# A decoder layer on eight cores: residual loaded into the accumulators, a seventh weight slab, split first loads, the last norm in halves

## The reference

```python
b_gate, c_gate, hc, q, k, v, g = split(x @ w_in)           # 512 columns each
y_conv = b_gate * causal_short_conv(c_gate * hc, conv_w)   # 3 taps
q, k = rotary(q), rotary(k) * 128 ** -0.5
o = chunkwise_retention(q, k, v)                           # 4 heads, chunks of 128
y_ret = silu(g) * head_group_norm(o)
x = layer_norm(ALPHA * x + concat([y_conv, y_ret]) @ w_out)
ff = square(relu(x @ w_ff1)) @ w_ff2                       # 1024 -> 4096 -> 1024
ple = sigmoid(x @ w_ple_gate) * (p @ w_ple_proj)
x = layer_norm(ALPHA * x + ff + ple)
```

## Time and profile before

| what | value |
|---|---|
| median of 6 runs | 891.23 us |
| profiled execution | 891.71 us |
| its span (first to last instruction, slowest core) | 890.1 us |
| spans of the eight cores | 880.8 to 890.1 us |
| mean granted TensorE clock of the cores | 0.972 to 0.980 |
| TensorE busy | 810.1 us (91%) |
| VectorE (DVE), ScalarE (ACT), GpSimd (POOL) busy | 443.9, 277.6, 147.4 us |
| moved by DMA | 128.41 MB, mean 144 GB/s |

### The profile page before, as it was taken

One profiled execution on the slowest core, in us unless ns is written; L12 is line 12 of the kernel. 1 busy time (PEld: TensorE's weight loads), 2 busy tenths in 40 slices (PEclk: granted clock), 3 DMA queues, 4 the chain that ended last, 5 costly groups with the idle time before them and its releaser, 6 DMA issues.

```text
span 890.1 us, 12563 instructions; the slowest of 8 cores (880.8 to 890.1 us)
## 1 busy us (share of the span) xinstructions
PE 810.1 (91%) x4088; PEld 375.8 (42%) x4088; DVE 443.9 (50%) x696; ACT 277.6 (31%) x500; POOL 147.4 (17%) x205
## 2 busy tenths in 40 slices
PE   1999999999878999659999999999999999999990
PEld 0444444444444444214444444444444444444440
DVE  4458544556754345124268454437653436844153
ACT  2222236545566333002234312214320322431010
POOL 2000145544454200001001000101100101100010
PEclk9999999999999999859999999999999999999995
DMA  8993599962367999968476877567787667784311
GB/s 134 218 173 53 104 165 108 123 108 59 48 103 135 147 195 183 178 126 144 139 176 182 220 181 180 125 167 171 201 197 189 134 151 140 215 208 108 88 48 47
DMA packets 21999, 128.41 MB, mean 144 GB/s; under 512 B 2800, under 2 KB 2928, under 8 KB 10224
## 3 DMA queue, kind: packets, MB, share of 16 engines
q0 software_dynamic: 11856, 83.37, 55.0%
q1 hardware_dynamic: 10080, 44.25, 14.8%
HBM read 194.19 MB, written 18.87 MB: 239 GB/s over the span
## 4 chain that ended last, share of the span: by engine, by line
PE 67%; DMA 11%; DVE 7%; issue 5%; ACT 4%; POOL 4%; DVEq 0%; ACTq 0%; POOLq 0%; SPq 0%
PE ps L194 65%; DMA xin_117<-x 5%; DMA ring_104<-w_gate 4%; DMA wc_59<-wc 2%; ACT sqj L223 2%; DVE lnst L673 2%; POOL st_51 L201 1%; DVE xacc_119 L201 1%; PE psT L198 1%; DVE xacc_118 L201 1%; ACT xacc_119 L223 1%; POOL lnst L201 1%; DVE ra_80 L201 1%; ACT xacc_118 L223 1%; DVE ob_93 L201 0%
## 5 line engine op out<-in xcount | busy, mean ns | idle before, releaser
L223 ACT ACTIVATE xacc_119<-xacc_119,lnst 128x1024 f32<-128x1024 f32 x16 | 19.8, 1240 | 133.9 <-DVE lnst L212 133.9
L194 PE MATMUL ps<-ring_106,hT 128*128 128x512 bf16 x160 | 42.7, 429 | 15.5 <-DVE xacc_119 L212 15.5
L201 POOL TENSOR_TENSOR lnst<-lnst,neghalf 128x1 f32<-128x1 f32 x32 | 17.9, 561 | 163.9 <-DVE lnst L205 163.8
L201 DVE TENSOR_TENSOR hT<-ps,tR_128 128x512 bf16<-128x512 f32 x43 | 29.6, 689 | 29.9 <-ACT tR_128 L223 29.8
L194 PE MATMUL ps<-ring_108,hT 128*128 128x512 bf16 x192 | 43.2, 379 | 0.7 <-DVE xacc_119 L212 0.7
L194 PE MATMUL ps<-ycat,ring_107 128*128 128x512 bf16 x192 | 43.6, 383 | 0.0
L194 PE MATMUL ps<-ring_109,hT 128*128 128x512 bf16 x192 | 43.2, 379 | 0.0
L194 PE MATMUL ps<-ycat,ring_106 128*128 128x512 bf16 x192 | 42.9, 379 | 0.3 <-DMA ring_106<-w_ff 0.3
L201 DVE TENSOR_TENSOR hT<-ps,tR_129 128x512 bf16<-128x512 f32 x42 | 28.9, 689 | 28.4 <-ACT tR_129 L223 28.3
L201 DVE TENSOR_TENSOR hT<-ps,tR_127 128x512 bf16<-128x512 f32 x43 | 29.6, 689 | 26.1 <-ACT tR_127 L223 24.5
L223 ACT ACTIVATE tR_127<-ps 128x512 f32<-128x512 f32 x43 | 25.7, 598 | 53.2 <-PE ps L194 49.0
(11 more groups left out here) (268 smaller groups left out, 1459.4 us busy)
## 6 DMA issues: line engine op xcount, KB each, us to landing
ring_106<-w_ff POOLq DMA_DIRECT2D x11, 1024.0 KB, 9.7
ring_108<-w_ff POOLq DMA_DIRECT2D x11, 1024.0 KB, 9.2
ring_104<-w_ff POOLq DMA_DIRECT2D x10, 1024.0 KB, 9.4
ring_109<-s_ff SPq DMA_DIRECT2D x9, 1024.0 KB, 5.3
s_ff<-w_ff POOLq DMA_DIRECT2D x8, 1024.0 KB, 29.8
ring_105<-s_ff SPq DMA_DIRECT2D x8, 1024.0 KB, 5.7
ring_107<-s_ff SPq DMA_DIRECT2D x7, 1024.0 KB, 5.2
ring_107<-w_ff POOLq DMA_DIRECT2D x4, 1024.0 KB, 20.9
```

The source lines that it names most:

```text
L194: self.P.op("pe", lambda e: e.matmul(out, lhsT=lhsT, rhs=rhs, start=start, stop=stop, skip_group_check=skip), reads, writes)
L201: self.P.op(eng, lambda e: e.tensor_tensor(out=out, in0=in0, in1=in1, op=op), reads, writes)
L223: self.P.op("act", lambda e: e.activation(out=out, in_=in_, func=func, **kw), reads, writes)
```

## The change

`xin` is used by tile 0 alone. For tiles 1 to 3, x is loaded by SP into `xacc` itself, one DMA per block of 128 rows, and `mix_part` works in place; tile 1's loads are issued before the channel stage, those of tile tt + 2 from `gen_out(tt, bi)` behind the output DMAs that free the rows. The ring gets a seventh buffer on the bytes of `xin`, and loads go up to 6 slabs ahead. Four casts are put ahead of the first three slab loads. The first two `xT` tiles and `wc` groups are loaded in quarters along the contraction (`wc` is laid out anew for that), and the first four conv steps take their matmuls in the order of the pieces, the third and fourth step in alternation. For the last tile the norm is made by four fused operations on half rows, with statistics of the first half made after its own sum and one output DMA per half, on SP and on ACT.

```diff
-    NR = 6
-    ring_off = [o_wc, o_wc + 8 * KB, o_wc + 16 * KB, o_xT + 16 * KB, o_xT + 24 * KB, o_sin]
+    NR = 7
+    ring_off = [o_wc, o_wc + 8 * KB, o_wc + 16 * KB, o_xT + 16 * KB, o_xT + 24 * KB, o_sin,
+                o_cb + 8 * KB]
...
-        cast(xT[0][:], xTd[0], ("xT", 0), ("xT", 0))
-        cast(wc[0][:], wcd[0], ("wc", 0), ("wc", 0))
...
+        for k in range(4):
+            load_part(0, 0, k)
+            load_part(1, 0, k)
+        for kind, i in ((1, 1), (0, 1), (1, 2), (1, 3), (0, 2), (0, 3)):
+            for k in range(len((xT_res, wc_res)[kind][i])):
+                load_part(kind, i, k)
...
-        slab_buf = [0, 1, 2, 3, 0, 1, 4, 5]
+        slab_buf = [0, 1, 2, 3, 0, 1, 6, 4, 5]
         while len(slab_buf) < len(slab_list):
-            slab_buf.append(slab_buf[-6])
+            slab_buf.append(slab_buf[-7])
...
+            order = [(gi, kc) for gi in (2, 1, 0) for kc in range(8)]
+            if by_piece:
+                order = [(gi, kc) for kc in range(8) for gi in (2, 1, 0)]
+            step = 3 if len(units) > 1 else 24
+            for o in range(0, 24, step):
+                for tt, j, par in mms:
+                    nx, nw = len(xT_res[tt]), len(wc_res[j])
+                    for gi, kc in order[o:o + step]:
+                        bk = 3 * par + 2 - gi
+                        h.mm(ps[bk][:], wc[j][:, kc, gi, :], xT[tt][:, kc, :], kc == 0, kc == 7,
+                             [wc_res[j][kc * nw // 8], xT_res[tt][kc * nx // 8]], [RP[bk]])
+            for m in mms:
+                conv_rest(*m)
...
-        for tt, j in ((0, 0), (0, 1), (1, 0), (1, 1), (0, 2), (1, 2), (0, 3), (1, 3)):
-            conv(tt, j)
+        conv((0, 0), by_piece=True)
+        conv((0, 1), by_piece=True)
+        conv((1, 0), (1, 1), by_piece=True)
+        for tt, j in ((0, 2), (1, 2), (0, 3), (1, 3)):
+            conv((tt, j))
...
+        issue_casts(4)
         prefetch(3)
-        issue_casts(3)
...
+        def load_x(tt, bi):
+            b = tt * 4 + bi
+            h.dma("sp", x1v(tt, bi), x[b * 128:(b + 1) * 128, :], ("xl", bi), [], [x1r(tt, bi)])
...
-            h.stt(x1v(tt, bi)[:, cols], xin[i][:], ALPHA, ps[bank][:], ALU.mult, ALU.add,
-                  [("xin", i), RP[bank]], [x1r(tt, bi)])
+            xs, xr = x1v(tt, bi)[:, cols], x1r(tt, bi)
+            if tt == 0:
+                k = 2 * bi + hf
+                xs, xr = xin[k % 4][:], ("xin", k % 4)
+            h.stt(x1v(tt, bi)[:, cols], xs, ALPHA, ps[bank][:], ALU.mult, ALU.add,
+                  [xr, RP[bank]], [x1r(tt, bi)])
...
-                        bg.add(gen_out(tt, bi))
+                        bg.add(gen_last(tt, bi))
...
+        def gen_last(tt, bi):
...
+            last_stats(tt, bi, 1)
+            yield
+            P.op("dve", lambda e: e.bn_aggr(out=mv, in_=lnst[:, 4 + bi, 0:12]), [rl], [rl])
+            h.ts("dve", rstd, mv[:, 1:2], LN_EPS, ALU.add, [rl], [("rstd", bi)])
+            h.tt("pool", rstd, rstd, neghalf[:, 0:1], ALU.pow, [("rstd", bi), "neghalf"],
+                 [("rstd", bi)])
+            yield
+            halves = [(buf[:, k * 512:(k + 1) * 512], (rb, "half", k)) for k in range(2)]
+            for k in range(2):
+                v, r = halves[k]
+                h.stt(v, v, mv[:, 0:1], lnt[2][:, k * 512:(k + 1) * 512], ALU.subtract, ALU.mult,
+                      [rb, rl, "ln2w"], [r])
+                yield
+            for k in range(2):
+                v, r = halves[k]
+                h.stt(v, v, rstd, lnt[3][:, k * 512:(k + 1) * 512], ALU.mult, ALU.add,
+                      [r, ("rstd", bi), "ln2b"], [r])
+                h.dma(("sp", "act")[k], out[b * 128:(b + 1) * 128, k * 512:(k + 1) * 512], v,
+                      ("outl", bi, k), [r], [("out", b, k)])
+                yield
...
         def gen_out(tt, bi):
...
+            if tt < 2:
+                for k in ([], [0], [1], [2, 3])[bi]:
+                    load_x(tt + 2, k)
             yield
 
+        for bi in range(4):
+            load_x(1, bi)
         for tt in range(4):
```

More of the change, by code:

```diff
@@ L276, in build_nc @@
     pos = din("pos", [128, NB], I32)
-    wcd = din("wc", [4, 128, 3, 8, 128])
+    wcd = din("wc", [4, 128, 8, 3, 128])
     wqkvg = din("wqkvg", [4, 128, 8, 512])
@@ L339, in build_nc @@
     x1b = [at("x1b%d" % i, [128, D], BF16, o_x1b + i * 2 * KB, ("x1b", i)) for i in range(2)]
-    xT = [at("xT%d" % i, [128, 8, 512], BF16, o_xT + i * 8 * KB, ("xT", i)) for i in range(4)]
-    wc = [at("wc%d" % i, [128, 3, 8, 128], BF16, o_wc + i * 6 * KB, ("wc", i)) for i in range(4)]
+    xT_res = [[("xT", i, k) for k in range((4, 4, 1, 1)[i])] for i in range(4)]
+    wc_res = [[("wc", i, k) for k in range((4, 4, 1, 1)[i])] for i in range(4)]
+    xT = [at("xT%d" % i, [128, 8, 512], BF16, o_xT + i * 8 * KB, xT_res[i]) for i in range(4)]
+    wc = [at("wc%d" % i, [128, 8, 3, 128], BF16, o_wc + i * 6 * KB, wc_res[i]) for i in range(4)]
     ub = [at("ub%d" % i, [128, 514], F32, o_cb + i * 2080, ("ub", i)) for i in range(4)]
@@ L416, in build_nc, with load_part @@
         P.op("dve", lambda e: e.memset(neghalf[:], -0.5), [], ["neghalf"])
-        cast(xT[0][:], xTd[0], ("xT", 0), ("xT", 0))
-        cast(wc[0][:], wcd[0], ("wc", 0), ("wc", 0))
[L420 to L425, removed]
+        def load_part(kind, i, k):
+            t, src, res = ((xT, xTd, xT_res), (wc, wcd, wc_res))[kind]
+            n = 8 // len(res[i])
+            cast(t[i][:, k * n:(k + 1) * n], src[i][:, k * n:(k + 1) * n], res[i][k], res[i][k])
+        for k in range(4):
[4 more added lines that the diff above has]
+                load_part(kind, i, k)
         for i, (t, n) in enumerate(((wG, "wG"), (wQ, "wQ"), (wK, "wK"))):
@@ L464, in prefetch, with use_slab @@
                     cast(ring[i][:], wsrc[nm][0][g], ("ring", i), ("ring", i))
-        def use_slab(nm, g, ahead=5):
+        def use_slab(nm, g, ahead=6):
             k = slab_n["use"]
@@ L509, in build_nc, with conv, conv_rest @@
         it = [0]
-        def conv(tt, j):
-            par = it[0] % 2
-            it[0] += 1
+        def conv(*units, by_piece=False):
+            mms = []
+            for tt, j in units:
+                par = it[0] % 2
+                it[0] += 1
+                mms.append((tt, j, par))
+            order = [(gi, kc) for gi in (2, 1, 0) for kc in range(8)]
[11 more added lines that the diff above has]
+                conv_rest(*m)
+        def conv_rest(tt, j, par):
             bH, bC, bB = [3 * par + i for i in range(3)]
[L515 to L518, removed]
             u = ub[j]
@@ L566, in proj @@
                 h.mm(ps[b][:], xT[n // 4][:, kc, ck(n)], w[:, kc, :], kc == 0, kc == 7,
[L567 removed]
+                     [wn] + xT_res[n // 4], [RP[b]])
             return b
@@ L690, in gen_ln @@
             yield
-        xorder = [(bi, hf) for bi in range(4) for hf in range(2)]
-        xorder += [(4 * tt + bi, hf) for tt in range(1, 4) for hf in range(2) for bi in range(4)]
-        xn = {"load": 0, "use": 0}
         def load_xin(k):
[L697 to L704, removed]
+            if k < 8:
+                bi, hf = k // 2, k % 2
+                h.dma("sp", xin[k % 4][:], x[bi * 128:(bi + 1) * 128, hf * 512:(hf + 1) * 512],
+                      ("xin", k % 4), [], [("xin", k % 4)])
+        def load_x(tt, bi):
+            b = tt * 4 + bi
+            h.dma("sp", x1v(tt, bi), x[b * 128:(b + 1) * 128, :], ("xl", bi), [], [x1r(tt, bi)])
         def x1v(tt, bi):
@@ L713, in mix_part @@
             b = tt * 4 + bi
-            i = xn["use"] % 4
-            assert xorder[xn["use"]] == (b, hf) and xn["use"] < xn["load"]
-            xn["use"] += 1
             cols = slice(hf * 512, (hf + 1) * 512)
@@ L720, in mix_part @@
                      [("ycat", b), rs], [RP[bank]])
-            h.stt(x1v(tt, bi)[:, cols], xin[i][:], ALPHA, ps[bank][:], ALU.mult, ALU.add,
-                  [("xin", i), RP[bank]], [x1r(tt, bi)])
-            if xn["use"] % 8 <= 4 and xn["use"] % 8 > 0:
-                load_xin(1)
+            xs, xr = x1v(tt, bi)[:, cols], x1r(tt, bi)
[4 more added lines that the diff above has]
+                  [xr, RP[bank]], [x1r(tt, bi)])
+            if tt == 0:
+                load_xin(k + 4)
         def gen_ln1(tt, bi):
@@ L742, in ff1_group @@
             if fc % 4 == 0:
-                ff1["slab"] = use_slab("ff1", fc // 4, 5 if tt or fc > 4 else 0)
+                ff1["slab"] = use_slab("ff1", fc // 4, 6 if tt or fc > 4 else 0)
             slab, rs = ff1["slab"]
@@ L801, in build_nc @@
                 slabs0 = [use_slab("wout", g, 0) for g in range(2)]
-                load_xin(4)
+                for k in range(4):
+                    load_xin(k)
             if 8 <= t < 12:
@@ L810, in build_nc @@
             if t == 12:
-                prefetch(6)
+                prefetch(7)
             if t == 16:
-                prefetch(8)
+                prefetch(9)
             if t % 2 == 0:
```

(13 more changed lines are left out.)

8 lines of the change are left out of this document (3 added, 5 removed).

## The result

The kernel after takes 858.22 us in the median (856.16 to 893.03, 10 runs) beside 891.56 us for the one before (20 runs): a ratio of 0.963 with an interval of 0.9616 to 0.9645. The forecast was 857 us, its own range 854 to 861. The profiled execution took 856.0 us (before 891.7), with a span of 854.5 us on the slowest core, number 3 as before; the eight spans lie between 849.7 and 854.5 us, and the mean granted clock is 0.987 to 0.992. In some executions of the kernels, the one before among them, the cores of one die show a lower granted clock (means down to 0.81), and the ratios leave these out; in the last pair of experiments cores 0 to 3 did so (0.94 to 0.96) in every execution, so that pair is compared by the spans of cores 4 to 7, without one execution in which these were slow too.

The account below looks back on a forecast made before the run. TensorE was taken as the engine to follow, stopped by late x loads beside a full DMA. Terms 29.8 + 5.4 - 1.0 = 34.2 us off 891.7 give 857.5, median 857 us; own range 854 to 861, wider range 851 to 866.

Parts of the forecast that it names:

- Residual: Loading x of tiles 1 to 3 into the accumulators removes TensorE's idle waits and half clock: 29.8 us gained.
- The step to ff2 slab 0: TensorE would reach the first ff2 slab of tile 0 at 367 us, with the slab in time.
- the waits on `x1b`: 2.0 us of transposes waiting for the next tile's norm, expected to go once the x wait is gone.
- Seventh slab and casts: Extra ring buffer and earlier casts pay for the 1.2 us gate wait already counted; nothing added.
- a slab wait between 320 and 400 us: Sign of being wrong: slabs named as what TensorE waits for in that stretch.
- Start: Split loads and first four conv steps: loss of 1 us, with 2.7 us of gain and 3 of loss as ends.
- a bank wait: In conv steps three and four TensorE stands 4 us for the third bank of step two.
- The charge of nothing for the cut: At the start, cutting input loads into quarters was taken not to make them land later: 0 us.
- Rival (a): Quarters land late: each of twelve further pieces holds the input stream up 0.57 us, 864 us; chance 7%.
- Rival (d): The start gains instead, the pair of conv steps ending with `wc` 2: 853 to 854 us; chance 12%.
- Last norm: Last tile's norm in fused halves: blocks no longer queue up, chain after the last sum 5.5 us; gain 5.4 us.
- rival (c): Denser program loses clock over the whole matmul time: slower than before, 900 us at clock 0.95; chance 3%.

Follow-up runs that it names:

- the last pair of experiments: Changed kernel with steps three and four in sequence, wVf after wc 3, x late: 849.2 us; with whole loads, old order, wVf after wc 3: 853.5 us.
- the run with late x: The changed kernel with tile 1's four x loads issued at tile 0's gate phase instead of before the channel stage: 856.87 us, ratio 0.9575.
- the kernel with both edits: The changed kernel with conv steps three and four in sequence and wVf loaded after wc 3 instead of wc 1: 852.13 us, ratio 0.9528.

## Why the prediction was right, and where its steps were not

*Residual, 29.8 us.* Measured 27.0 in the middle and 4.0 behind it, 31.0 us together; the seventh slab has its share in this sum (next paragraph). The step to ff2 slab 0, forecast at 367 us, came at 366.95. That the waits on `x1b` would go with the x waits held: TensorE's list from 424 us on is empty. Right for a reason I had only half: the prediction gave the late request as the cause of the stop, and the run with late x shows that loads in the same full stretch, twice as large and all asked for at once, are in time but for 1.8 us on DVE. As far as these runs show, the stop was the price of twice as many loads at the same 7 us each, half of which had to wait for a buffer.

*Seventh slab and casts, 0 us.* This term was mis-sized. "If this cover were gone, the 1.2 us would come back": without it 3.4 to 4.4 us come back. The prediction followed the ff2 slabs, which the change brings nearer, and not the ff1 slabs, ahead of which it puts 2 MB of x. The total did not suffer, since 29.8 us were counted with that cover in place; the residual alone gives 23 us. One of the prediction's signs of being wrong, a slab wait between 320 and 400 us, came in small: 0.2 to 1.8 us on five of the eight cores.

*Start, -1.0 us.* Measured -1.15, by the mechanism foreseen: a bank wait (3.0 us against about 4), then half clock (2.7 us against about 2), the fifth step at 43.4 us (41 to 46). The first matmul came at 11.84 us and not near 9, but the first step ended at 21.3 us (20.5 to 21.8), as the last quarter set it. The charge of nothing for the cut was too kind. `wc` 2, issued behind the sixteen pieces, landed at 42.7 us instead of 40.1. These rows of the kernel after, DMA issues from 11 us on, answer to the earlier trace rows; by POOL's timeline its issue came at 11.22 us instead of 3.83.

```profile
wc_61<-wc POOLq DMA_DIRECT2D x1, 768.0 KB, 31.5
```

So the stream is 2.6 us later on this core (0.7 to 3.2 us on the eight), where the earlier trace rows gave 0. On core 3 the bank wait hid it. On cores 0, 1 and 6 the fifth step waited for `wc` 2 itself, by 0.5 to 2.7 us. Rival (a) was thus partly true, at some third of its price. The 2.0 us for each DMA that the prediction took from the Trainium skill, DMA: Bandwidth & Descriptors, section Anatomy of one DMA, would give an estimated 24 us without overlap; the trace shows a ninth of that. Rival (d), a start that gains, did not come in the kernel after; the kernel with both edits shows that it could have: 852.1 us, not far from the 853 to 854 given for it.

*Last norm, 5.4 us.* Measured 5.8 in the two spans and 5.5 to 7.3 by undoing it; the chain from the last sum took 4.7 us where 5.5 was forecast. The power beside the fused halves takes 0.92 us instead of 0.56, but ends before its user wants it.

*Loss of clock, rival (c).* The dense stretches kept 1.00, and the mean rose on every core.

The total, 35.7 us in the profiled executions against 34.2 forecast, is a matter of small misses (+1.2, -0.15, +0.4). The residual's +1.2 hides that its 31.0 us are the work of two parts: alone it gives 23, and the seventh slab with the earlier casts, priced at nothing, brings most of the rest. The medians differ by 33.3 us: the profiled execution of the kernel after lies 2.2 us below its median, that of the kernel before 0.5 us above.

## What to carry to other kernels

Before costing a moved load by its own lateness, look for what stands behind it in the queue at its new place: here 2 MB of early x would have taken back some 4 us in slabs, and the extra buffer with the earlier casts kept them. An early start pays as far as the next resource in line allows: with the banks and the second queue's 2 MB in its way it gave nothing, and with the order of steps and loads changed together it gave 3.6 us, where the order of steps alone lost 3 to 4 (by the times; the ratios overlap). Where a small load lands late beside a full queue, count its rows before its bytes.

## What was not expected of the hardware

Beside a full POOL queue SP's loads landed 6.4 to 8.4 us after one another whether they held 256 KB in rows of 2 KB or 512 KB in rows of 4 KB. Sixteen quarter loads in place of four whole ones made the stream 0.7 to 3.2 us later on the eight cores, at most 0.3 us for each further load. POOL's power of 128 values took 0.92 to 0.93 us in the four last blocks beside DVE's scalar_tensor_tensor on two tiles in SBUF, and 0.56 us with DVE idle, as in the last block before:

```profile
874.15 0.56 POOL L201 TENSOR_TENSOR lnst<-lnst,neghalf 128x1 f32<-128x1 f32 x1 [1.80 <-DVE lnst L205]
```

The Trainium skill, GPSIMD Engine Reference, section Specifications, has POOL share its SBUF interfaces with DVE, with contention from DVE instructions with two SBUF inputs; this agrees.
